# Latent attention layer: gate units behind both units of keys, gate evictions right behind their unit, output units ahead of the last rotary one

## What is computed

```python
def mla_mixer(h, w_in, q_norm_g, kv_norm_g, w_uq, w_ukv, w_out, cos, sin):
    c_q, c_kv, k_rope, g = split(h @ w_in)              # 256, 128, 64, 2048 columns
    q = rmsnorm(c_q, q_norm_g) @ w_uq                   # 16 heads of 128 + 64 (rotary)
    kv = rmsnorm(c_kv, kv_norm_g) @ w_ukv               # 16 heads of 128 (keys) + 128 (values)
    q_nope, q_rope = q[..., :128], apply_rope(q[..., 128:], cos, sin)
    k_nope, v = kv[..., :128], kv[..., 128:]
    for i in range(8):                                  # blocks of 128 queries, causal
        s = (q_nope[i] @ k_nope.T + q_rope[i] @ k_rope.T) * scale
        o[i] = softmax(mask(s)) @ v
    return (o * silu(g)) @ w_out
```

## Time and profile before

| | us |
|---|---|
| median of 3 runs | 2589.19 |
| lowest, highest | 2583.03, 2590.29 |
| the profiled execution | 2590.05 |
| its span, first to last instruction | 2588.1 |
| mean granted TensorE clock, share of full | 0.968 |

### The profile page before, as it was taken

One profiled execution on the slowest core, in us unless ns is written; L12 is line 12 of the kernel. 1 busy time (PEld: TensorE's weight loads), 2 busy tenths in 40 slices (PEclk: granted clock), 3 DMA queues, 4 the chain that ended last, 5 costly groups with the idle time before them and its releaser, 6 DMA issues. The chain is left out here.

```text
span 2588.1 us, 43259 instructions
## 1 busy us (share of the span) xinstructions
PE 2365.7 (91%) x17364; PEld 1335.5 (52%) x17364; DVE 1569.3 (61%) x2220; ACT 1348.4 (52%) x2029; POOL 462.5 (18%) x418
## 2 busy tenths in 40 slices
PE   8999989987888888989888999999998799999987
PEld 4667654444544454445444455555454345776643
DVE  5566665765655556656546566666666465667654
ACT  4434443445545444444433677777778543444432
POOL 0000111122111102011012223233223210011011
PEclk9999999998899999999989999999999899999998
DMA  3011112214334334424331221121211121111113
GB/s 116 26 42 50 34 34 91 75 48 89 74 75 83 77 79 79 86 65 95 80 86 57 59 58 34 50 58 50 58 41 34 41 91 34 35 50 33 34 59 120
DMA packets 197721, 160.31 MB, mean 62 GB/s; under 512 B 160114, under 2 KB 161394, under 8 KB 197524
## 3 DMA queue, kind: packets, MB, share of 16 engines
q1 hardware_dynamic: 193428, 153.35, 22.4%
q0 software_dynamic: 4096, 4.20, 0.7%
HBM read 98.79 MB, written 4.19 MB: 40 GB/s over the span
## 5 line engine op out<-in xcount | busy, mean ns | idle before, releaser
L240 PE MATMUL psum<-h_hi,w_hi 128*128 128x512 f16 x1128 | 431.7, 383 | 35.7 <-ACT mla_silu_g L285 18.4
L241 PE MATMUL psum<-h_lo,w_hi 128*128 128x512 f16 x1128 | 431.5, 382 | 0.0
L242 PE MATMUL psum<-h_hi,w_lo 128*128 128x512 f16 x1128 | 431.3, 382 | 0.0
L2340 DVE SCALAR_TENSOR_TENSOR w_lo<-wf,w_hi 128x1024 f16<-128x1024 f32 (+3 forms) x194 | 231.1, 1199 | 138.8 <-ACT w_hi L2335 138.7
L256 PE MATMUL psum<-w_hi,h_hi 128*128 128x128 f16 x1504 | 256.9, 219 | 0.0
L258 PE MATMUL psum<-w_hi,h_lo 128*128 128x128 f16 x1504 | 256.5, 219 | 0.0
L257 PE MATMUL psum<-w_lo,h_hi 128*128 128x128 f16 x1504 | 256.5, 219 | 0.0
L1619 ACT ACTIVATE ssum<-psum,mla_neg_top 128x128 f32<-128x128 f32 (+7 forms) x128 | 94.7, 740 | 298.3 <-DVE mla_neg_top L1526 298.3
L1097 POOL TENSOR_TENSOR sb_al<-sb_zc,sb_ah 128x256 f16<-128x256 f32 (+2 forms) x96 | 166.2, 1732 | 373.0 <-ACT sb_ah L1062 373.0
L2335 ACT ACTIVATE w_hi<-wf 128x1024 f16<-128x1024 f32 (+3 forms) x194 | 187.0, 975 | 39.7 <-PE psum L242 19.6
L240 PEld LDWEIGHTS psum<-h_hi,w_hi 128*128 128x128 f16 x1128 | 111.3, 99 | 159.1 <-issue 42.9
(11 more groups left out here) (325 smaller groups left out, 5859.7 us busy)
## 6 DMA issues: line engine op xcount, KB each, us to landing
wf<-in_gla_out SPq DMA_DIRECT2D x32, 512.0 KB, 3.5
wf<-in_sb_in SPq DMA_DIRECT2D x32, 512.0 KB, 3.5
wf<-in_mla_out SPq DMA_DIRECT2D x20, 512.0 KB, 3.9
wf<-in_gla_v SPq DMA_DIRECT2D x16, 512.0 KB, 3.5
wf<-in_gla_g SPq DMA_DIRECT2D x16, 512.0 KB, 3.5
wf<-in_mla_gate SPq DMA_DIRECT2D x16, 512.0 KB, 3.6
wf<-in_sb_out SPq DMA_DIRECT2D x16, 512.0 KB, 3.5
xT<-in_x_T SPq DMA_DIRECT2D x16, 256.0 KB, 5.1
```

The costliest lines, as they stand in the source:

```text
L240: pe.matmul(out, wh[:, w], act_hi[:, k, tok], start=(i == 0), stop=False)
L241: pe.matmul(out, wh[:, w], act_lo[:, k, tok], start=False, stop=False)
L242: mm = pe.matmul(out, wl[:, w], act_hi[:, k, tok], start=False, stop=(i == last))
L2340: dve.scalar_tensor_tensor(out=self.w_lo[s % Layer.NSPLIT][:, 0:cols], in0=self.wf[s % Layer.NLOAD][:, 0:cols], scalar=W_SCALE, in1=self.w ...
```

## The change

In `weave_even` a gate's `gz` follows its unit at once rather than at the next gap. In `ORDER` the second string is new: in heads 4 to 14 both units of keys stand ahead of the gate units, the gate units alternate with those of values, and the output units stand ahead of the last rotary one.

```diff
 def weave_even(main, filler, cost):
         while k < len(filler) and spent * gaps < weight * work:
             out.append(filler[k])
             spent += cost(filler[k])
             k += 1
+        while 0 < k < len(filler) and filler[k][0] == "gz":
+            out.append(filler[k])
+            k += 1
     return out + filler[k:]
...
     ACC = [5, 6, 7]
-    ORDER = "uuuuuugrgr", "uuguuguuxrxrxx"
+    ORDER = "uuuuuugrgr", "uuuuguguxxrxxr"
```

## The result

| us | before | after |
|---|---|---|
| median | 2589.1 | 2607.55 |
| lowest, highest | 2583.03, 2590.29 | 2606.35, 2608.14 |
| the profiled execution | 2590.05 | 2606.35 |
| its span | 2588.1 | 2604.5 |
| mean granted TensorE clock | 0.968 | 0.963 |

The changed kernel takes 1.0075 times the time of the kernel before, 95% interval 1.0058 to 1.0093: 18 us slower. 2610 was predicted. The edits add three lines to `weave_even`, so every line of the file behind them is 3 higher than in the rows of before: L240 is now L243, L285 L288, L619 L622, L1442 L1445, L1548 L1551.

A forecast was written before the change was run, and what follows sets the result against it. A ring of VectorE and ScalarE, not TensorE, was taken to set the pace in heads 4 to 15. Terms 18.6 - 2.75 + 3.75 + 1.2 = +20.8 us gave 2610 us against the median, range 2574 to 2620.

The forecast's parts named there:

- The ring: Heads 4 to 15: VectorE and ScalarE alternate on maximum, exp, high half, low half, setting the pace except at L1548 waits.
- Rival 1: Head starts: slack takes the new waits, L1548 isn't late and only savings count; 2569 us, chance 0.2.
- KN.1's wait: Start of heads from 4 on: second unit of keys waits 2.5 us for the first query unit's bank.
- L1548 late by 2.7 us at full clock, 4.4 with a spell at half: Even heads 4 to 14: VectorE's product of the finished half head comes late; half-clock stretch adds 1.7 us.
- 1.3 us given back in steps 2 and 3: Even heads 4 to 14: 0.5 us from one eviction fewer, 0.8 us from value evictions; leaves +3.1 us, six times.
- Rotary: Steps 4 to 7 of five even heads with a rotary slab: moved rotary units net -0.55 us each, -2.75 together.
- Second heads: Odd heads 5 to 13, steps 0 to 3: two key-unit waits and a half-clock spell, +0.75 us each, +3.75 together.
- Heads 0 to 3: Order kept, only gates move up a gap: +1.2 us, bounds -5 and +8.
- The loop in heads 4 to 14: Steps 2 and 3: value evictions no longer stand behind a gate block twice, 0.8 us saved a head.
- What was to be seen: Gate waits near nothing, key-unit waits about 2.5 us, L1548's wait 8 us or more a pair, clock 0.5, pair 105 us.
- The chances: Whole kernel's measured time: slower 0.58, within 0.3% 0.22, faster 0.20.
- Rival 2: Head starts: new waits come but TensorE keeps 2.4 GHz behind them; 2589 us, no change, chance 0.2.

The follow-up runs named there:

- busy_wait_old_order: Kernel before, with the three matmuls of the first unit of keys issued four times over in heads 4 to 14, extra results thrown away; 2587.88 us.
- gate_bank: Kernel before plus prompt gate evictions in heads 4 to 15, output units ahead of the last rotary one, first gate unit in bank 3; 2564.53 us.
- order_only: Kernel before with only the new order string, the interleaving loop left as it was; 2609.81 us.
- rotary_back: Changed kernel with the rotary units put back among the output units; 2609.79 us.
- key_bank: Changed kernel with the second unit of keys of heads 5 to 15 in bank 1, empty in steps 0 to 3; 2597.16 us.
- loop_only: Kernel before with only the loop edit, a gate's eviction right behind its unit, old order of units; 2582.39 us.
- busy_wait: Changed kernel with the three matmuls of the first unit of keys issued four times over in heads 4 to 14, extra results thrown away; 2594.25 us.

## Why the prediction was right

The time was right within 3 us, and that is in part luck, because the parts had errors that cancel: +20.8 was made of 18.6, -2.75, 3.75 and 1.2; measured are 9.65, -2.18, 4.67 and 4.58.

- **The ring sets the pace: right.** busy_wait_old_order (21 us of TensorE's work for nothing) shows it, and in gate_bank the span followed VectorE's wait (11.6 and 11.8 us). Rival 1, slack that takes the new waits, falls with the L1548 wait: 12.9 us before, 27.5 after.
- **KN.1's wait: right.** 2.5 us predicted, 2.41 to 2.42 measured, 0.79 us behind the start of QN.0's low half (0.80 predicted from the earlier trace rows). KN.0's in second heads was put at about 3 us and is 3.90.
- **L1548 late by 2.7 us at full clock, 4.4 with a spell at half: right, both.** Head 6 shows 2.53, head 8 4.21. **The step that failed is that the spell comes each time.** It came in three of six first heads. 1.68 us of clock in three heads instead of 1.7 in six is 5.2 us less.
- **1.3 us given back in steps 2 and 3: near,** 1.55 in head 6 and 1.54 in head 8. Three heads like 6 and three like 8 would give 11.0; head 4 (2.07) and head 14 (0.27) stand 0.6 and 0.7 below theirs, and that is the 9.65 in place of 18.6.
- **Rotary: right in the net,** -0.55 a head against -0.44; order_only and rotary_back put it on this move alone. But the terms as printed (2.1 + 1.0 + 1.2 - 1 - 2 x 0.6) add up to +2.1, not to -0.55: they leave out what leaves step 4 with QR.0. Measured in head 6, from maximum 4 on, are -2.13, -0.27, -0.62 and +2.59.
- **Second heads: right in size,** +0.75 against +0.93 on average, from 0.40 to 2.78 where they lose and -0.39 in head 11. Much of the spread is the clock: at half for 8.9 us in head 13 where the kernel before has none, for 6.8 in head 11 where it has 5.8. And the share of the two waits was misread. Both were charged; rotary_back cuts KN.0's and KN.1 starts no sooner, key_bank keeps KN.0's 3.94 us and takes KN.1's away, and the heads win 10.4 us. The bound without a spell was given as -1.35; 0.75 less half of the 4 us taken is -1.25.
- **Heads 0 to 3: too small,** 1.2 for 4.58. The +2.1 for a gate block that no longer lies beside QR's work came in twice (2.25 each) as it was priced, out of four times allowed for. What I took off for heads 1 and 3 (1 to 1.5, four times) came twice, at 1.67. 1.1 us of the rest lies between maxima 1 and 2 of head 3 and is there in order_only and gate_bank too, which don't touch heads 0 to 3; it is not the change's.
- **The loop in heads 4 to 14 was under-priced under the old order only.** Alone it is worth 10 us there (loop_only). The prediction looked at VectorE behind the gate block and found 0.8 a head, 4.8 in all. From order_only to the changed kernel the first heads gain 6.2, but 3.4 of that are two spells that the second trace doesn't have (heads 6 and 10); in heads 8 and 12, which have one in both, the gain is 0.35 each.
- **What was to be seen.** Of the signs named, the gate's waits at nothing, the waits at KN and the clock came. L1548's wait did not grow to 8 us a pair: it is 2.02 and 2.60 in heads 6 and 7. Work that VectorE now does ahead of it (both KN evictions) and the wait for the scores of step 1 fill the delay. The delay was predicted well; the wait is a poor measure of it. The pair is 102.8 or 105.2 us, 105 was given.
- **The chances.** 0.2 and twice 0.02 are 0.24 for a time within 0.3%, not 0.22, which leaves 0.18 for faster.

Rival 2, the clock that stays up, is right for three of the six heads; it has the same mechanism and lacks only the spell. busy_wait is its test: without the spells in heads 8 and 12 and with a smaller wait in the second heads 2594.25 is left, not the 2589 of that rival; head 4 and four of the second heads still have spells in it.

## What to carry to other kernels

Where a ring of two other engines sets the pace, price an edit of TensorE's order by when it hands over, at the few places where the ring takes something from it, not by TensorE's waits. Compare two traces head by head with the granted clock beside them: here a spell more or less is 1.7 us, as much as most of the edits are worth a head. Before moving a unit, ask whose bank it inherits and when that bank's low half is written: KN.1 moved from a bank long free to one that VectorE had just begun to empty. Then look for a bank that another stage leaves empty in those steps; that was worth more than any order of the units.

## What the runs showed of the hardware that was not expected

- **One wait, two clocks.** Behind KN.1's wait of 2.41 or 2.42 us, at the same place of the program, the granted clock is 1.00 in heads 6, 10 and 14 and 0.54 in heads 8 and 12. The wait ahead of that one doesn't decide it: 1.03 us in head 8, which falls, 1.07 in head 14, which doesn't. What decides is open; a fall costs 1.7 us (4.21 less 2.53).
- **More matmuls, less time.** Nine throw-away matmuls in each of eleven waits: 2607.55 to 2594.25 us. Real work moved there wasn't tried.
- **A long wait in the shadow of a shorter one.** KN.0's 3.9 us in the second heads could shrink to 1.19 (rotary_back) without bringing KN.1 forward, whose own wait grew from 2.29 to 3.55 us; with KN.1's gone and KN.0's kept (key_bank) a head wins 2 us, part of it by the clock. Between the two waits, 3.4 us at the lower clock, TensorE had three matmuls to do:

```profile
896.20:899.60 3.40, 1.18 (x3) 0.19 (x3) 2.32 (x5) 1.43 (x4) 2.28 (x1) 0.54 0.88 174
```
